# Two raw landing areas for streamed weight chunks in place of four, in a two-layer decoder trunk

## The reference, cut to what matters

```python
h = x
hn = rmsnorm(h, norm_g[0])                       # layer 0: retention, 8 heads
q, k, v, gate = split(hn @ ret_w_in)             # widths 2048, 2048, 4096, 4096
o = groupnorm(decayed_scores(q, k) @ v)
h = h + (silu(gate) * o) @ ret_w_out
hn = rmsnorm(h, norm_g[1])                       # layer 1: sparse attention, 16 heads in 4 groups
q, six key/value parts, gates, z = split(hn @ nsa_w_in)
o = gates-weighted sum of compressed, selected and window attention
h = h + (silu(z) * o) @ nsa_w_out
out = rmsnorm(h, final_g)
```

## Time and profile before

| what | us |
|---|---|
| median of 3 runs (lowest, highest) | 1242.73 (1242.27, 1243.19) |
| the profiled execution | 1243.32 |
| its span, from first to last instruction | 1241.5 |
| PE busy in the span | 1227.8 (99%) |
| DVE busy | 719.6 (58%) |
| ACT busy | 558.7 (45%) |
| transfers | 223.82 MB, mean 180 GB/s |
| PE's mean granted clock | 0.998 of full |

### The profile page before, as it was taken

One profiled execution on the slowest core, in us unless ns is written; L12 is line 12 of the kernel. 1 busy time (PEld: TensorE's weight loads), 2 busy tenths in 40 slices (PEclk: granted clock), 3 DMA queues, 4 the chain that ended last, 5 costly groups with the idle time before them and its releaser, 6 DMA issues.

```text
span 1241.5 us, 16047 instructions
## 1 busy us (share of the span) xinstructions
PE 1227.8 (99%) x6208; PEld 1027.0 (83%) x6208; DVE 719.6 (58%) x826; ACT 558.7 (45%) x732; POOL 41.9 (3%) x53
## 2 busy tenths in 40 slices
PE   8999999999999999999999999999999999999997
PEld 7788888888888888888888888888888787887875
DVE  6554465464564564565465476644547576775675
ACT  6643343343343344344343445334345555563553
POOL 0000000000000000000000010000000000000000
PEclk9999999999999999999999999999999999999999
DMA  9955555455555555555555476645543355444422
GB/s 323 362 174 198 175 175 197 169 190 181 171 200 178 176 187 188 179 181 195 169 192 181 170 253 203 223 153 203 171 154 136 118 167 171 137 162 141 138 73 97
DMA packets 130110, 223.82 MB, mean 180 GB/s; under 512 B 7200, under 2 KB 40496, under 8 KB 129680
## 3 DMA queue, kind: packets, MB, share of 16 engines
q1 hardware_dynamic: 127904, 215.77, 51.3%
q0 software_dynamic: 1728, 7.10, 1.8%
q10 hardware_dynamic: 432, 0.31, 0.1%
HBM read 221.06 MB, written 2.10 MB: 180 GB/s over the span
## 4 chain that ended last, share of the span: by engine, by line
PE 94%; DMA 3%; ACT 1%; issue 1%; DVE 1%; SPq 1%; POOL 0%; POOLq 0%; ACTq 0%
PE acc L1048 23%; PE acc L1023 16%; PE acc L1025 16%; PE acc L1024 16%; PE acc L1049 11%; DMA w_raw<-in_ret_w_in 3%; PE side L1189 2%; PE side L1275 2%; PE side L1023 1%; PE side L1025 1%; PE side L1024 1%; PE side L1262 1%; PE side L1277 1%; PE side L1214 1%; PE side L1105 1%
## 5 line engine op out<-in xcount | busy, mean ns | idle before, releaser
L691 DVE TENSOR_TENSOR w_lo<-w_raw,w_hi 128x2048 fp32r<-128x2048 f32 x196 | 448.3, 2289 | 337.8 <-ACT w_hi L457 335.4
L457 ACT CAST w_hi<-w_raw 128x2048 fp32r<-128x2048 f32 x196 | 372.8, 1908 | 362.9 <-PE acc L1025 242.6
L1048 PE MATMUL acc<-hT,w_hi 128*128 128x512 f32 x1216 | 431.3, 399 | 0.0
L1049 PE MATMUL acc<-hT,w_lo 128*128 128x256 f32 x1216 | 339.4, 279 | 0.0
L1048 PEld LDWEIGHTS acc<-hT,w_hi 128*128 128x128 f32 x1216 | 228.3, 188 | 54.8 <-issue 1.1
L1049 PEld LDWEIGHTS acc<-hT,w_lo 128*128 128x128 f32 x1216 | 229.1, 188 | 0.7
L1023 PE MATMUL acc<-w_hi,hT 128*128 128x512 f32 x576 | 225.2, 391 | 0.9 <-DVE qT L741 0.9
L1025 PE MATMUL acc<-w_hi,hT 128*128 128x512 f32 x576 | 224.4, 390 | 0.0
L1024 PE MATMUL acc<-w_lo,hT 128*128 128x512 f32 x576 | 224.2, 389 | 0.0
L1023 PEld LDWEIGHTS acc<-w_hi,hT 128*128 128x128 f32 x576 | 108.2, 188 | 23.5 <-DVE w_lo L691 1.2
L1025 PEld LDWEIGHTS acc<-w_hi,hT 128*128 128x128 f32 x576 | 108.1, 188 | 22.7
(11 more groups left out here) (166 smaller groups left out, 857.5 us busy)
## 6 DMA issues: line engine op xcount, KB each, us to landing
w_raw<-in_ret_w_in SPq DMA_DIRECT2D x184, 512.0 KB, 4.4
w_raw<-in_nsa_w_in SPq DMA_DIRECT2D x112, 512.0 KB, 4.3
w_raw<-in_ret_w_out SPq DMA_DIRECT2D x64, 512.0 KB, 4.3
w_raw<-in_nsa_w_out SPq DMA_DIRECT2D x32, 512.0 KB, 4.7
w_raw<-in_ret_w_in SPq DMA_DIRECT2D x12, 256.0 KB, 5.7
res<-in_x SPq DMA_DIRECT2D x2, 1024.0 KB, 11.3
arena<-in_nsa_cmp_w_k POOLq DMA_DIRECT2D x1, 2048.0 KB, 12.2
arena<-in_nsa_cmp_w_v POOLq DMA_DIRECT2D x1, 2048.0 KB, 11.7
```

Of the source, the lines that this page charges most:

```text
L457: act.copy(w_hi[:, s, :, :], w_raw[:, s, :, :]).then_inc(hi_done, 1)
L691: dve.tensor_tensor(w_lo[:, s, :, :], w_raw[:, s, :, :], w_hi[:, s, :, :].bitcast(F32), ALU.subtract).then_inc(lo_done, 1)
L1048: pe.matmul(parts[m][:, :], w_hi[:, s, i, w], hT[:, k, :, :], start=(k == 0), stop=False)
L1049: ins = pe.matmul(parts[m][:, 0:S], w_lo[:, s, i, w], hT[:, k, 0, :], start=False, stop=(k == KT - 1))
```

## The change

A new constant RAW = 2 sizes `w_raw`; `w_hi` and `w_lo` keep four slots. Chunk n now lands in raw slot n mod 2, and its request waits for the low part of chunk n-2. The same rule takes the place of the waits for landings at the start: the pieces of chunks 2 and 3 wait for the low parts of the pieces of chunks 0 and 1 whose places they take, and chunks 4 to 6 for `lo_done`. `gained` is laid out over the smaller tensor.

```diff
 RING = 4
+RAW = 2
...
-        w_raw = sb("w_raw", [P, RING, KPC, COLS])
+        w_raw = sb("w_raw", [P, RAW, KPC, COLS])
...
-        gained = w_raw[:, :, 0:TT, :]
+        gained = w_raw[:, :, :, :].rearrange("p r k n -> p (r k n)").rearrange("p (j t n) -> p j t n", j=CG, t=TT)
...
             def chunk(q, s, halves):
 
-                if not known(q, 0):
-                    sp.wait_ge(lo_done, 4 * q + s - 3)
+                sp.wait_ge(lo_done, 4 * q + s + 1 - RAW)
                 for to, src in halves:
                     sp.dma_start(to, src).then_inc(raw_in[s], 16)
 
             def by_rows(s, w, k0, col):
-                return [(w_raw[:, s, 2 * i:2 * i + 2, :], w[:, bass.ds(k0 + 2 * i, 2), bass.ds(col, COLS)]) for i in range(2)]
+                return [(w_raw[:, s % RAW, 2 * i:2 * i + 2, :], w[:, bass.ds(k0 + 2 * i, 2), bass.ds(col, COLS)]) for i in range(2)]
...
-                            landed = {(2, 0): (raw_in[0], 32), (2, 1): (w_piece[3], 32), (3, 0): (raw_in[1], 32), (3, 1): (w_piece[4], 32)}.get((c, p))
+                            landed = {(2, 0): (lo_piece, 2), (2, 1): (lo_done, 1), (3, 0): (lo_piece, 4), (3, 1): (lo_done, 2)}.get((c, p))
...
                     elif c < 8:
-                        if known(h, 0) and c < 7:
-                            sp.wait_ge(*((raw_in[2], 32), (w_piece[5], 32), (raw_in[3], 32))[c - 4])
                         if known(h, 0) and c == 7:
...
-                act.copy(w_hi[:, s, :, :], w_raw[:, s, :, :]).then_inc(hi_done, 1)
+                act.copy(w_hi[:, s, :, :], w_raw[:, s % RAW, :, :]).then_inc(hi_done, 1)
...
-                dve.tensor_tensor(w_lo[:, s, :, :], w_raw[:, s, :, :], w_hi[:, s, :, :].bitcast(F32), ALU.subtract).then_inc(lo_done, 1)
+                dve.tensor_tensor(w_lo[:, s, :, :], w_raw[:, s % RAW, :, :], w_hi[:, s, :, :].bitcast(F32), ALU.subtract).then_inc(lo_done, 1)
```

More of the change, by code:

```diff
@@ L318, in by_rows @@
             def by_rows(s, w, k0, col):
-                return [(w_raw[:, s, 2 * i:2 * i + 2, :], w[:, bass.ds(k0 + 2 * i, 2), bass.ds(col, COLS)]) for i in range(2)]
+                return [(w_raw[:, s % RAW, 2 * i:2 * i + 2, :], w[:, bass.ds(k0 + 2 * i, 2), bass.ds(col, COLS)]) for i in range(2)]
             def by_columns(s, w, k0, col_a, col_b):
-                return [(w_raw[:, s, :, i * DK:(i + 1) * DK], w[:, k0:k0 + KPC, bass.ds(c, DK)]) for i, c in enumerate((col_a, col_b))]
+                return [(w_raw[:, s % RAW, :, i * DK:(i + 1) * DK], w[:, k0:k0 + KPC, bass.ds(c, DK)]) for i, c in enumerate((col_a, col_b))]
             def ret_inputs(h):
@@ L338, in ret_inputs @@
                             for i in range(2):
-                                sp.dma_start(w_raw[:, c, a:z, i * DK:(i + 1) * DK], ret_in[:, ks, i * D:i * D + DK]).then_inc(w_done, 16)
+                                sp.dma_start(w_raw[:, c % RAW, a:z, i * DK:(i + 1) * DK], ret_in[:, ks, i * D:i * D + DK]).then_inc(w_done, 16)
                     elif c < 4:
@@ L478, in first_high @@
                     act.wait_ge(raw_in[j] if z == KPC else w_piece[WHOLE[j] + p], 32)
-                    act.copy(w_hi[:, j, a:z, :], w_raw[:, j, a:z, :]).then_inc(hi_done if z == KPC else hi_piece, 1)
+                    act.copy(w_hi[:, j, a:z, :], w_raw[:, j % RAW, a:z, :]).then_inc(hi_done if z == KPC else hi_piece, 1)
             def first_squares(t):
@@ L713, in first_low @@
                     dve.wait_ge(*piece_done(j, p, hi_piece, hi_done, j + 1))
-                    dve.tensor_tensor(w_lo[:, j, a:z, :], w_raw[:, j, a:z, :], w_hi[:, j, a:z, :].bitcast(F32),
+                    dve.tensor_tensor(w_lo[:, j, a:z, :], w_raw[:, j % RAW, a:z, :], w_hi[:, j, a:z, :].bitcast(F32),
                                       ALU.subtract).then_inc(lo_done if z == KPC else lo_piece, 1)
```

## The result

| | before | after |
|---|---|---|
| median (lowest, highest), 4 runs each | 1242.58 (1242.27, 1243.19) | 1257.68 (1255.81, 1257.79) |
| the profiled execution | 1243.32 | 1257.59 |
| its span | 1241.5 | 1255.8 |
| PE's mean granted clock | 0.998 | 0.994 |

What follows compares the result with a forecast made beforehand. PE was taken as the bound, with the DMA queues beside it up to 61 us. 1243.3 us plus 4.1 and 4.0 is 1251.4, less 0.6 for the median gives 1250.8 us, range 1246.5 to 1256.

Steps and rivals of the forecast that it cites:

- the mechanism and its two places: Requests two lows later stall PE at the start (+4.1 us) and the retention layer's end (+4.0); both as worked out 0.55.
- the end of the retention layer: Chunk 128, requested beside POOL's 2.5 MB, lands 4.9 us late for its high; PE waits for residual adds, +4.0 us.
- the heads and the sparse layer: Highs 2.3 us late at each head's output projection, up to 4 late in the sparse layer; cost 0.
- The rival that the borders stall too: Head borders have 0.8 us slack; landings 1.5 later cost 0.7 six times, as much in the sparse layer: 1257, chance 0.09.
- the +4.1 of the start: Up to the first matmul on v: high 10 starts at 57.8, 4.1 us after its former 53.69, and v follows.
- the first link: At the start, chunk 4 is asked for when low 2 ends at 21.05 and lands near 26.2, about as before.
- The price of a lone request: Any chunk requested on idle queues: data is there 5.0 us after the low that frees its slot.
- its high came 4.6 after high 7: At the start, chunk 8 shares queues with POOL's 1.1 MB of decay tables as before, so it lands at 48.5.
- The upper bound of +6: Upper bound of the start's cost, +6 us, if low 7 misses PE's start and the queue is slower too.
- the clock at 0: PE's clock after stalls: 0 taken as likeliest; rival, half a chunk's work at half clock, 2.7 us more, 1253.5, chance 0.10.
- The prediction's own sign of being wrong: Listed signs against it: PE idle at L1048 at each head, L1146 no later, or a granted clock below 1.
- The rival that two slots are enough: Circle of 9.2 us is shorter than two chunks on PE (about 11), both stalls hidden: 1241.5 to 1243, chance 0.10.

Runs made afterwards that it cites:

- The first experiment: Changed kernel with four raw slots again, every request still waiting for the low part of chunk n-2: 1256.65 us, ratio 1.0109.
- the two that split it in time: Four raw slots, requests late as in the changed kernel only for chunks 2 to 11 (1251.63 us, ratio 1.0068) or only from chunk 12 (1248.87 us, ratio 1.0049).
- sparse load later: Changed kernel with POOL's 2.5 MB for the sparse layer issued behind the second norm's token factor: 1255.51 us, ratio 1.0096.
- small tables after chunk 4: Changed kernel with POOL's first two loads (192 KB) issued only when chunk 4 has landed: 1257.01 us, ratio 1.0111.
- the kernel with all repairs: Changed kernel with residual rows before chunk 6, both squares before high 6, v ahead of chunk 10, sparse load in pieces: 1246.96 us, ratio 1.0029.
- rows before chunk 6: Changed kernel with the residual rows (2 MB) asked for before chunk 6 in place of after it: 1256.23 us, ratio 1.0099.
- load in pieces: Changed kernel with POOL's 2 MB w1 in four pieces, one behind each of lows 126 to 129, two small loads after low 130: 1251.29 us, ratio 1.0069.
- late requests from chunk 12: Four raw slots, start's waits as before the change, chunks from 12 on waiting for the low of n-2: 1248.87 us, ratio 1.0049.

## Why the prediction was right and wrong

**Right: the mechanism and its two places.** Requests two lows ahead cost at the start and where POOL's 2.5 MB drain, and nowhere else. The first experiment shows that the time of the requests does it, not the tensor; the two that split it in time leave room for no third place within their intervals.

**Right: the end of the retention layer.** Forecast 4.0, measured 4.33, by the steps given: 12.8 us for the chunk, the adds a round of 6.7 apart, PE waiting for the first and the third.

**Right: the heads and the sparse layer.** The high was 2.3 late, as worked out, and cost 0. In the sparse layer five highs came 3.5 to 4.8 late, none with an idle PE. The rival that the borders stall too gave 1257, the number that came out, and it would have been luck: the profile refutes its reason, since the offset from 64 to 741 us doesn't move. (By its own terms, 0.7 six times and as much again, it should have read 1259.)

The sum was 8.1 and the profile shows 14.3. Of the 6.2 us between them 3.5 are the clock and 2.8 the start.

**Wrong: the +4.1 of the start, in the landings of chunks 4 and 8.** "Chunk 4 is asked for when low 2 ends at 21.05 and lands near 26.2" was the first link; it was asked for at 21.25 and landed at 28.30. The price of a lone request came from 707 us; at the start it holds in three executions (4.98 to 5.21) and not in seven (6.2 to 7.1). But a late chunk 4 explains only a part. Two later experiments leave chunks 5 to 10 as they are in the changed kernel, and in them chunk 4 landed as forecast:

| | chunk 4 landed | chunk 7 | chunk 8 | high 10 starts | v later than 61.29 |
|---|---|---|---|---|---|
| forecast | 26.2 | 44.0 | 48.5 | 57.8 | 4.1 |
| changed kernel | 28.30 | 46.32 | 50.87 | 60.61 | 6.93 |
| sparse load later | 26.48 | 43.57 | 49.91 | 59.60 | 5.91 |
| small tables after chunk 4 | 26.41 | 43.66 | 49.70 | 59.39 | 5.71 |

So the late chunk 4 is worth 1.0 to 1.2 of the 2.8 us, from single executions. With it on time the term that fails is "its high came 4.6 after high 7", for chunk 8: it comes 6.0 to 6.3 after, as ACT's timeline of the kernel with the later sparse load shows.

```profile
43.59 1.91 ACT L455 CAST w_hi<-w_raw 128x2048 fp32r<-128x2048 f32 x1 [5.85 <-DMA w_raw<-in_ret_w_in]
49.93 1.91 ACT L455 CAST w_hi<-w_raw 128x2048 fp32r<-128x2048 f32 x1 [4.43 <-DMA w_raw<-in_ret_w_in]
```

Chunk 8 was asked for 1.1 and 1.4 us ahead of POOL's tables in these two, 2.2 ahead in the changed kernel and 7.0 ahead in the kernel before. That the tables, now nearly level with it, hold it back is likely and not tested. Another 0.3 is chunk 10's own landing, 5.4 us after its request where 5.1 was forecast. The upper bound of +6 rested on low 7 and on a slower queue, and didn't cover the 6.93. That PE begins chunk 4 1.76 us later was missed as well; it is part of the 6.93.

**Wrong: the clock at 0.** The forecast took it as a rival at 0.10 with a price of 2.7, on the ground that no idle of before up to 1.21 us had lowered it. The longest of before is in fact 1.86, ahead of a piece of chunk 1:

```profile
13.38 2.09 PE L1078 MATMUL acc<-hT,w_hi 128*128 128x512 f32 x8 [1.86 <-ACT w_hi L479]
```

The forecast was for one of over 5: the row that was nearest in kind was far away in size. The prediction's own sign of being wrong, a granted clock below 1, is what the profile shows. Measured: 1.80 us behind 6.34 idle and 1.68 behind 2.18. The Trainium skill's rule in "TensorE: Matmul & The Clock Gate", Part 1, that an idle array falls to 1.2 GHz and must be busy again to get 2.4 back, is borne out by this trace: the clock is 0.50 over 68 to 72, with PE at work. How long an idle time it takes can't be told from these runs: one of 2.82 us left the clock up and one of 1.81 was followed by the lower level, both in the kernel with all repairs. Together the two clock terms are 3.5 and the start 2.8, and 8.1 + 3.5 + 2.8 = 14.4 is the 14.3 measured. The end came out 0.3 above its forecast and the rest 0.4 below, and the two cancel.

**The rival that two slots are enough** falls by all runs. The sentence of the Trainium skill behind it ("Trainium Kernel Development and Optimization", Best Practices, "Double-buffer for performance") holds in the loop, where two areas cost 0 us over 680 us, and fails at the two places where landing, high (1.9) and low (2.3) together take longer than two chunks on PE, about 11 us: 9.1 + 4.2 for chunk 8 and 12.8 + 4.2 for chunk 128; even with those repaired the ratio was 1.0029.

## What to carry to other kernels

The depth of a prefetch buffer is set by its worst place, not by its steady circle: look for the start and for every large transfer on another queue, and take the landing time from the rows with the same neighbours. Before giving up slots, cut a large load into pieces that fit between the requests; here that alone gave back some 6 of 15 us (ratio 1.0069 in place of 1.0116). And where a change makes PE idle by some us in one piece, price the clock as part of the stall and not as an afterthought.

## What the runs showed of the hardware that was not expected

- **A stall of 6.3 us cost 1.8 us more than its length, one of 2.2 us cost 1.7 more**, and filling the first with useless matmuls gave the 1.8 back. The price doesn't go by the length of the stall: behind the wait for v it was 2.8 us for an idle time of 5.92, 2.5 for 7.13 and 1.3 for 6.41 (rows before chunk 6, sparse load later, load in pieces). It goes by how much of the stretch at the lower level falls on work, and is about half of that: 3.9 us of work cost 1.8, 6.0 cost 2.8, 5.4 cost 2.5, 2.8 cost 1.3. The stretches lasted 3.4 to 10.2 us. One that came ahead of a wait for data cost nothing in the end (32.64 to 36.05 in the first experiment).
- **The same idle time doesn't always lower the clock.** 2.18 us at the end of the layer did in the changed kernel and in four others, and didn't with four areas (ratio 1.0109) or with late requests from chunk 12. 2.46 us at 33.04 left it up in the changed kernel; 2.26, 2.46, 2.06 and 2.11 there lowered it in four others. With all repairs 2.82 us left it up. What decides between them was not tried. It makes a difference of 1 to 2 us between kernels that do the same.
- **One request takes 5.0 to 7.1 us to land at the same place in eleven near-equal kernels**, mostly in step with the issue of its second half (0.48 to 1.41 us). A load of 2.5 MB on another queue delays a chunk that is asked for behind it to 12.8 and 13.8 us, at the two places where it was put whole; with its 2 MB in four pieces the chunk landed in 5.0.
